# Attention banks read ahead of the selection rounds, fewer filler products, and a token table in two parts

## The reference, cut to what matters

```python
# mixer of the first block: a sparse half and a stick-breaking half
score = einsum(relu(q_idx . k_idx), w_idx); _, idx = top_k(score, 128)   # per query
logits over those keys -> softmax -> @ v_a -> @ w_uv                      # y_a
z = q_b . k_b / 8                                                         # 8 heads, causal
log_a = log_sigmoid(z) + reverse_cumsum(log_sigmoid(-z)) - log_sigmoid(-z)
y_b = exp(log_a) @ v_b
merged = sigmoid(gate_a) * (y_a @ w_o_a) + sigmoid(gate_b) * (y_b @ w_o_b)

# mixer of the second block: gated recurrence hm, differential attention ha, then [hm, ha] @ w_out

# experts of the second block: 32 experts in 4 groups, two experts per token
y = sum over the two experts of weight * ((silu(x @ w_gate[e]) * (x @ w_up[e])) @ w_down[e])
```

## Time and profile before

| what | value |
|---|---|
| median of 3 runs | 1993.67 us (1993.01 to 1994.95) |
| the profiled execution's own time | 1993.76 us |
| span in its profile | 1991.9 us |
| granted TensorE clock, mean | 0.992 |
| busy: PE, DVE, ACT | 96%, 52%, 35% |
| chain that ended last | PE 73%, DVE 10%, DMA 10%, ACT 5% |

### The profile page before, as it was taken

How to read it: one execution, slowest core, us unless ns; L and a number is a source line. 1 busy time by engine, 2 the same in 40 slices (tenths; PEclk the granted TensorE clock), 3 DMA queues, 4 the chain that set the end, 5 groups by cost and what they waited for, 6 DMA issues and landing times.

```text
span 1991.9 us, 22020 instructions
## 1 busy us (share of the span) xinstructions
PE 1909.5 (96%) x8839; PEld 1380.6 (69%) x8839; DVE 1044.3 (52%) x1690; ACT 699.7 (35%) x1139; POOL 42.1 (2%) x67
## 2 busy tenths in 40 slices
PE   7999999998999989999999999999999999998998
PEld 6888888875778867888888878877676444443433
DVE  5443554467777886544334447565765333332333
ACT  5321323345556364332222234565542111111111
POOL 0000000100000001000000000000000000000000
PEclk9999999999999999999999999999999999999999
DMA  5323334134223304333233333222168999999997
GB/s 172 102 87 103 98 96 112 46 80 59 76 64 75 106 27 135 92 95 102 85 106 95 96 94 97 75 64 57 60 238 353 421 420 420 420 421 420 420 422 292
DMA packets 256302, 338.65 MB, mean 170 GB/s; under 512 B 10001, under 2 KB 218897, under 8 KB 232641
## 3 DMA queue, kind: packets, MB, share of 16 engines
q1 hardware_dynamic: 249744, 320.71, 46.9%
q0 software_dynamic: 5872, 15.41, 2.1%
q10 hardware_dynamic: 576, 1.05, 0.1%
HBM read 332.74 MB, written 8.39 MB: 171 GB/s over the span
## 4 chain that ended last, share of the span: by engine, by line
PE 73%; DVE 10%; DMA 10%; ACT 5%; issue 1%; SPq 0%; DVEq 0%; ACTq 0%
PE bank L183 72%; DMA large<-w_up 10%; PE bank L186 1%; ACT wH L189 1%; ACT p L189 1%; ACT T L189 1%; DVE PTL L195 1%; DVE y L195 1%; DVE p L198 0%; DVE score L201 0%; DVE score L219 0%; DVE st L207 0%; DMA stage<-w_gate 0%; ACT rr L189 0%; DVE top L216 0%
## 5 line engine op out<-in xcount | busy, mean ns | idle before, releaser
L183 PE MATMUL bank<-hH,wH 128*128 128x512 f32 x1096 | 433.8, 396 | 16.4 <-DVE stage0L L195 12.1
L183 PE MATMUL bank<-hL,wH 128*128 128x512 f32 x1096 | 428.3, 391 | 0.0
L189 ACT ACTIVATE wH<-stage 128x1024 fp32r<-128x1024 f32 (+3 forms) x231 | 228.4, 999 | 98.7 <-PE bank L183 84.6
L183 PE MATMUL bank<-large,xF 128*64 128x512 f32 x1024 | 236.6, 604 | 18.7 <-DMA large<-w_up 16.8
L183 PEld LDWEIGHTS bank<-hH,wH 128*128 128x128 f32 x1096 | 206.9, 189 | 62.2 <-DVE stage0L L195 12.1
L183 PEld LDWEIGHTS bank<-hL,wH 128*128 128x128 f32 x1096 | 206.9, 189 | 43.7 <-issue 1.7
L183 PEld LDWEIGHTS bank<-large,xF 128*64 128x64 f32 x1024 | 75.4, 139 | 150.2 <-issue 143.1
L183 PE MATMUL bank<-hidH,wH 128*128 128x512 f32 x352 | 137.4, 390 | 2.1 <-DVE stage2L L195 0.9
L183 PE MATMUL bank<-hidL,wH 128*128 128x512 f32 x352 | 137.0, 389 | 0.0
L195 DVE TENSOR_TENSOR yoL<-bank,yoH 64x512 fp32r<-64x512 f32 x64 | 44.1, 689 | 148.7 <-ACT yoH L189 147.7
L183 PE MATMUL bank<-large,hF 128*64 128x512 f32 x512 | 116.0, 595 | 0.0
(11 more groups left out here) (494 smaller groups left out, 3352.9 us busy)
## 6 DMA issues: line engine op xcount, KB each, us to landing
large<-w_gate SPq DMA_DIRECT2D x64, 1024.0 KB, 26.8
large<-w_up SPq DMA_DIRECT2D x64, 1024.0 KB, 26.7
large<-w_down SPq DMA_DIRECT2D x64, 1024.0 KB, 26.7
stage<-w_in SPq DMA_DIRECT2D x56, 512.0 KB, 4.1
stage<-w_gate SPq DMA_DIRECT2D x44, 512.0 KB, 3.7
stage<-w_up SPq DMA_DIRECT2D x44, 512.0 KB, 3.7
stage<-w_down SPq DMA_DIRECT2D x16, 512.0 KB, 3.5
stage<-w_out SPq DMA_DIRECT2D x12, 512.0 KB, 4.1
```

The lines of the kernel that those rows point to most:

```text
L183: return self.e.matmul(*a, **k) if self.e is not None else Nothing()
L189: return self.e.activation(*a, **k) if self.e is not None else Nothing()
```

## The change

In the first mixer the list is reordered: rounds of `topk` that stood between a projection and the read of its bank are moved behind the read, in equal number within each part of the list. The read of gate 7 before head 3 gets an `evict()` of its own ahead of `qk(2, 1)`. `b3(4)` moves behind `qk(3, 1)` and the split of head 5. `b1` of an even head waits only for the even k buffer. The constant products of `b1` go, those of `expand(0)` go from 13 to 6, and `values(0)` moves ahead of `logits(4)`. In the second mixer the weights are prepared three units early instead of two in one `fill`. For the experts, the table of token numbers becomes a product of its own that waits for fewer DVE operations, in bank 1, and the row scales and weights are a second product behind project(0,1), in bank 6. `extras` uses another tile. The second `fetch` no longer waits for `ei` but for `rs`. The transposes of blocks 2 and 3 move into the middle of down(0), and DVE's part of them ahead of that of down(0).

```diff
@@ mixer1
-                left.append(Step("split_qk", ..., y=gts.take(("qk", c, which)), ...))
+                left.append(Step("split_qk", ..., y=gts.take(("qk_odd", c) if which else ("qk", c)), ...))
             score(3, 1, low4)
-            topk(1)
             qk(0, 1, 7)
-            topk(1)
             evict()
-            topk(1)
+            topk(2)
             gate(5)
-            topk(2)
+            topk(3)
             b1(0)
...
             part("b1_max", 1)
-            topk(2)
-            evict()
             topk(1)
             part("b1_split", 1)
+            evict()
             b3(0)
-            topk(1)
+            b3_split(0)
             qk(1, 1, 7)
-            b3_split(0)
             evict()
             part("b2", 1)
-            topk(1)
+            topk(4)
             part("b2_exp", 1)
...
             part("b2_exp", 2)
             part("b2", 2)
+            evict()
             topk(1)
             part("b2_split", 2)
             b1(3)
             part("b1_log", 3)
             qk(2, 0, 6)
             b3(2)
-            topk(2)
             part("b1_max", 3)
+            topk(1)
+            part("b1_split", 3)
             evict()
             b3_split(2)
-            part("b1_split", 3)
-            topk(1)
             qk(2, 1, 7)
+            evict()
             part("b2", 3)
-            topk(1)
-            evict()
+            topk(3)
             part("b2_exp", 3)
...
             qk(3, 0, 6)
-            b3(4)
             qk(3, 1, 7)
-            b3_split(4)
             part("b1_max", 5)
             topk(1)
             part("b1_split", 5)
-            topk(1)
             evict()
+            b3(4)
+            b3_split(4)
             part("b2_exp", 5)
-            topk(1)
+            topk(2)
             part("b2_split", 5)
...
             turn_p(2)
+            values(0)
             logits(4)
             evict()
-            values(0)
@@ mixer2, fill
+                ahead[0] = AHEAD + (outs[0] == 6)
                 add_out(outs[0], 0, hm, ("hm", 3))
+                ahead[0] = AHEAD
@@ moe
-            M.xg.slots[1][1] = ("ei",)
+            M.xg.slots[1][1] = ("rs", 1)
...
             project(0, 0)
-            add(Step("table", bank=banks.take(("rs", 1))))
+            ids_bank = banks.take(("tokx",), 1)
+            add(Step("table", bank=ids_bank))
             add(Step("extras"))
...
             project(0, 1)
+            add(Step("table_shares", bank=banks.take(("rs", 1), 6)))
...
+                if n == 0:
+                    turn_x(2)
+                    steps[-1].inside = turned = steps[-1]
+                    fetch(2 + 2 * NGR)
                 down(n)
                 if n == 0:
-                    turn_x(2)
-                    fetch(2 + 2 * NGR)
+                    steps[-1].inside = turned
@@ PE
-                        keep_clock(s.banks[0], {0: 13}.get(n, 0))
+                        keep_clock(s.banks[0], {0: 6}.get(n, 0))
...
-                        keep_clock(s.z[0], {0: 9, 2: 7, 6: 9}.get(n, 0))
                         pe.wait_ge(*after("kb_zero", n % 2))
-                        pe.wait_ge(*after("qk", n // 2, 1))
+                        pe.wait_ge(*after("qk_odd" if n % 2 else "qk_even", n // 2))
+                        pe.wait_ge(*after("qk", n // 2))
...
                         for j in range(4):
                             u = s.units[j // 2]
+                            if j == 2 and s.inside:
+                                turn_pair(s.inside)
...
+                        pe.wait_ge(*after("ids_in",))
+                        for k in range(8):
+                            t = pe.matmul(s.bank.t[0:BLK, 0:NB + NX], R["J"][:, k, :], R["ge"][:, k, 0:NB + NX], ...)
+                    elif s.kind == "table_shares":
                         pe.wait_ge(*after("tables_in",))
-                            (64 x 3*47 from R["GE"][:, k, :, 0:NB + NX])
+                            (64 x 2*47 from R["GE"][:, k, 1:3, 0:NB + NX])
@@ DVE, choose / indices / extras
+                then(... R["ge"] = R["B"] * pair ..., "ids_in")
                 then(... R["Br"] = R["B"] * rcol ...)
-                then(... R["ge"] = R["B"] * pair ...)
                 shares(M)
-                then(... R["B"] = R["Br"] * w12 ..., "tables_in")
...
                 then(dve.tensor_copy(M.tokx[:, :], tf[:, NB:]), "tokx")
+                then(... R["B"] = R["Br"] * w12 ..., "tables_in")
...
-                (rs copied from the same bank)
+            def row_shares(s, M):   # waits for table_shares, then copies rs
...
-                le = R["GE"]...
+                le = M.oh[:, 0:NX * 32]...
+                dve.wait_ge(*after("mm", "first", 1))
```

More of the change, by code:

```diff
@@ L91, in __init__ @@
         self.kind = kind
-        self.key = self.unit = self.bank = self.y = self.gain = None
+        self.key = self.unit = self.bank = self.y = self.gain = self.inside = None
         self.n = self.m = self.k = self.i = 0
@@ L546, in qk @@
                 b = dense(steps, ("qk", c, which), wcols("w_in", (520, 1032)[which] + c * 128, 128), 8, h, ("qkf", c, which), None, n)
-                left.append(Step("split_qk", n=c, k=which, bank=b, y=gts.take(("qk", c, which)), held=("mm", "b1", 2 * c - 1) if c else ("sc", 3, 7)))
+                left.append(Step("split_qk", n=c, k=which, bank=b, y=gts.take(("qk_odd", c) if which else ("qk", c)), held=("mm", "b1", 2 * c - 1) if c else ("sc", 3, 7)))
             def vb_rows(kk):
@@ L1862, in mixer2_stage, with turn_pair @@
                         pe.matmul(s.bank.t[:, :], mat("ones"), s.sq.t[:, :], start=True, stop=True).then_inc(*did("drms", n))
+            def turn_pair(s):
+                pe.wait_ge(*after("xg%d" % s.xg.at, s.n))
+                rows = s.xg.t[:, :].rearrange("s (c p k) -> s c p k", c=2, k=4)
+                for c in range(2):
+                    free(s.banks[c])
+                    for k in range(4):
+                        t = pe.transpose(s.banks[c].t[:, 128 * k:128 * k + 128], rows[:, c, :, k], mat("ident"))
+                    t.then_inc(*did("mm", "xT", s.n, c))
             def expert_steps(steps):
@@ L1867, in expert_steps @@
                     if s.kind == "turn_pair":
[L1868 to L1874, removed]
+                        if not s.inside:
+                            turn_pair(s)
                     elif s.kind == "turn_x":
@@ L1983, in moe_stage @@
                     elif s.kind == "table":
+                        pe.wait_ge(*after("ids_in",))
+                        free(s.bank)
+                        for k in range(8):
+                            t = pe.matmul(s.bank.t[0:BLK, 0:NB + NX], R["J"][:, k, :], R["ge"][:, k, 0:NB + NX], start=k == 0, stop=k == 7)
+                        t.then_inc(*did("mm", "table"))
+                    elif s.kind == "table_shares":
                         pe.wait_ge(*after("tables_in",))
@@ L1987, in moe_stage @@
                         for k in range(8):
-                            t = pe.matmul(s.bank.t[0:BLK, 0:3 * (NB + NX)].rearrange("p (a n) -> p a n", a=3), R["J"][:, k, :], R["GE"][:, k, :, 0:NB + NX],
+                            t = pe.matmul(s.bank.t[0:BLK, 0:2 * (NB + NX)].rearrange("p (a n) -> p a n", a=2), R["J"][:, k, :], R["GE"][:, k, 1:3, 0:NB + NX],
                                           start=k == 0, stop=k == 7)
-                        t.then_inc(*did("mm", "table"))
+                        t.then_inc(*did("mm", "table_shares"))
                     elif s.kind == "fold":
@@ L2756, in mixer1_stage @@
                             dve.wait_ge(*after("qkh", n, 0))
-                            low(M.qb[1][:, :], s.y.t[:, :], M.qb[0][:, :], 0.125).then_inc(*did("qk", n, 0))
+                            low(M.qb[1][:, :], s.y.t[:, :], M.qb[0][:, :], 0.125).then_inc(*did("qk", n))
                         else:
@@ L3065, in indices @@
                 then(dve.tensor_copy(M.tokx[:, :], tf[:, NB:]), "tokx")
+                then(dve.tensor_tensor(R["B"][:, :, :], R["Br"][:, :, :], wide(R["w12"][:, :], [128, 8, NB + NX]), ALU.mult), "tables_in")
                 for half in range(2):
                     then(dve.tensor_copy(M.tp[BLK * half:BLK * half + BLK, :], tf[:, half:NB:2]))
+            def row_shares(s, M):
+                dve.wait_ge(*after("mm", "table_shares"))
                 for half in range(2):
-                    dve.tensor_copy(M.rs[BLK * half:BLK * half + BLK, :], s.bank.t[0:BLK, (NB + NX) * (1 + half):(NB + NX) * (2 + half)]).then_inc(*did("rs", half))
+                    dve.tensor_copy(M.rs[BLK * half:BLK * half + BLK, :], s.bank.t[0:BLK, (NB + NX) * half:(NB + NX) * (1 + half)]).then_inc(*did("rs", half))
             def extras(M):
-                le = R["GE"][:, :, :, :].rearrange("p a c b -> p (a c b)")[:, 0:NX * 32].rearrange("p (a b) -> p a b", b=32)
+                le = M.oh[:, 0:NX * 32].rearrange("p (a b) -> p a b", b=32)
+                dve.wait_ge(*after("mm", "first", 1))
```

(2 more changed lines are left out.)

6 lines of the change are left out of this document (2 added, 4 removed).

## The result

| what | before | changed |
|---|---|---|
| median | 1993.38 us (4 runs, 1993.01 to 1994.95) | 1980.68 us (4 runs, 1979.06 to 1981.36) |
| profiled execution, its span | 1993.76, 1991.9 us | 1979.06, 1977.1 us |

The ratio is 0.9932, with a 95% interval of 0.992 to 0.9945. The change is faster by 12.7 us where 18.7 were forecast; 1980.7 lies inside the range of 1970.5 to 1983 and 5.7 us above the point of 1975.0. The profiled execution is the fastest of the four and gained 14.8 us of span. In a later session of five executions the changed kernel had 1978.08 beside 1993.76. So the sum is first taken against the trace, and the rest is the spread between executions, which the experiments come back to.

What follows compares the result with a forecast made beforehand. PE, broken by DVE and ACT, was taken to bound the kernel up to 1749 us, then loads. Terms 14.1 + 1.0 + 0.9 + 2.7 = 18.7 us gave 1975.0 us; own range 1971 to 1979, stated range 1970.5 to 1983.

Steps and rivals of the forecast that it cites:

- the rivals: Clock falls (0.12), expert stage gives nothing (0.12), DVE bounds the head phase (1982 us, 0.08), slower by delayed splits (1998 us, 0.04).
- signs named for "wrong": Granted clock 0.5 behind any head's start, PE idle by T0L or T1L ahead of b2 or b3, or second DMA hole unchanged.
- the head phase: First mixer: heads start earlier as PE's waits, constants and slow clock go; 14.1 us gained, bounds about 5 and 16.4.
- DVE's walk: First mixer: DVE's new order walked with earlier durations; heads 0, 2, 4 at 499.0, 534.2, 571.3 us, earlier by 2.4, 5.3, 10.8.
- 36.2 us of PE lead to 607.5, DVE has k ready at 607.2: Step for head 6, first mixer: it starts at 607.5 us without waiting, 14.1 us earlier.
- first rival: First mixer: the clock falls at the even heads and at expand(0), price 4 x 2.2 plus 0.9, total 1984.7 us; chance 0.12.
- the row with 1.27 us: PE's wait for T1L ahead of head 1's b2 in the old trace; products still start 0.23 us apart after it.
- expand(0): First mixer: with values(0) first its product comes 2.5 us earlier, but the stretch is DVE's; 1.0 us gained, bounds 0 and 2.5.
- Second mixer: PE's 0.74 us wait for stage3L behind seven constants shortens, haL then sets it; 0.9 us gained, bounds 0 and 1.2.
- Experts: Expert stage: earlier table lets loads start sooner, closing most of the second DMA hole; 2.7 us gained, bounds 0.5 and 4.1.
- the first hole stays, the second closes but for 1.4 us: Low-rate stretches of the expert stage's DMA stream, 1520 to 1524 and 1528 to 1536 us, worth 3.1 and 4.1 us.
- the transposes inside down(0): Expert stage: they free PE of 3.4 us, counted as nothing because DMA is saturated from 1540 us on.

Runs made afterwards that it cites:

- e10: The kernel before with only the head phase of the change (order of reads and rounds, no constants in b1): 1984.06 us, ratio 0.995.
- e9: The kernel before with only the experts' part of the change (table in two parts, transposes inside down(0)): 1990.98 us, ratio 0.9985.
- e6: The changed kernel without the added reads of gate 7 ahead of qk(2,1): 1987.39 us, ratio 0.9964.
- e4: The changed kernel with the whole expert stage as before (one table of three parts, transposes behind down(0)): 1981.5 us, ratio 0.9943.
- e2: The changed kernel with b3(4) ahead of qk(3,1), its split ahead of head 5's, and one selection round moved behind the reads: 1979.91 us, ratio 0.993.
- e3: The changed kernel with values(0) behind logits(4) and 13 constants ahead of expand(0), as before: 1979.3 us, ratio 0.9933.
- e7: The changed kernel with the transposes of blocks 2 and 3 behind down(0) again, table still in two parts: 1981.76 us, ratio 0.9938.
- e1: The changed kernel again, no edit: 1978.08 us, ratio 0.993.
- e5: The changed kernel with the constant products of b1 again (9, 7 and 9 ahead of heads 0, 2 and 6): 1981.59 us, ratio 0.9945.
- e12: e11 without the added constants ahead of heads 2 and 4 and of the merge: 1974.24 us, ratio 0.9903.
- e11: e8 without the five constants at turn_p(3), and with the gate's read ahead of logits(4): 1975.24 us, ratio 0.9906.
- e8: e2 with constants added: 4 ahead of heads 2 and 4, 5 ahead of turn_p(3), 5 ahead of the merge; 1976.93 us, ratio 0.9916.

## Why the prediction was right, and where it was not

**Right in sign and in mechanism, with three of four terms within 1 us.** Where the gain lies (heads, then experts) is confirmed by each part alone: 9.8 us for the heads (e10) and 2.9 for the experts (e9). Undoing a part in a trace answers likewise: 6.1 us at head 4 (e6), 1.7 at the end of the stream (e4). But 1980.7 lies outside the forecast's own range of 1971 to 1979. It is inside the stated one only because that was widened for the rivals, two of which came true in part: DVE bound the even heads more than walked (idle of PE 0.38, 1.25, 1.24 and 1.92 us, forecast 0.7, 0.8, 0.7 and 0), and the clock fell in three places. One of the signs named for "wrong", a low clock behind a head's start, is there at head 6.

**The term that failed: the head phase, 14.1 forecast, 10.1 in the trace.** Up to head 4 DVE's walk holds within 0.6 us (gains 2.6, 5.0 and 10.2, forecast 2.4, 5.3 and 10.8). The step that failed is "36.2 us of PE lead to 607.5, DVE has k ready at 607.2". DVE's k was ready at 608.4, 1.2 later than walked, and I had walked only q and k: the bank that `b1(6)` writes is freed by a split which the diff moves behind exactly these reads. Of the 2.5 us lost at head 6 about 0.6 is head 4's own delay (PE is free at 608.1 in place of 607.5), 0.4 more is DVE's k, and 1.5 the bank. A lowered clock behind the 1.92 us of idle then cost 1.5 more (the gain falls from 11.6 at head 6 to 10.1). e2 moves that one split and gets the 1.5 of the bank and 1.4 of the clock back in its trace. In e3 and e7, with the same wait and no fall, head 7's product with v comes 12.1 and 12.4 us earlier than in the kernel before.

**The clock.** The first rival priced falls at the even heads and at expand(0). At heads 2 and 4, with 1.24 to 1.26 us of idle and no constants, the clock was 1.00 in all 17 cases of nine traces (changed, e1 to e5, e7, e10, e12), and at head 2 of e6 too. At head 6, with 1.92 to 1.94 us, it fell in five of seven (changed, e1, e4, e6, e10; not in e3 and e7). So there the argument from the row with 1.27 us held, and what failed was the length of the idle that I had foreseen at head 6. Behind the heads the rival was right where it spoke of expand(0): 0.62 in 688 to 692. There, where PE has less to do, shorter idles were enough: 1.24 us in e11, and at the merge 1.38 to 1.40 us in four of twelve traces (changed, e6, e7, e9). By the rule of the Trainium skill that was weighed (TensorE: Matmul & The Clock Gate, A second HAM failure mode: psum-queue depth-cycling) brief idles between groups, frequent enough, would do it. The traces agree in the sparse half, with idles of 0.8 to 1.7 us every few us; in the dense head phase idles of 1.25 us did not do it and single ones of 1.9 mostly did. That constants guard against it isn't shown: e5 has them and head 7's product comes 2.7 us later, e12 has none ahead of the heads and is the steadiest.

**expand(0): 1.0 forecast, about 0.6 over eleven traces.** Its product comes 12.7 us earlier where the heads gave 10.1, but most of it is only that the wait moves: 1.6 us for the gate's bank behind it, which no term had. e11 and e12 take it away.

**Second mixer: 0.9 forecast, 0.9 measured** (18.88 us from the last norm's products at 1456.25 and 1446.34 to the first with ha, now 18.00).

**Experts: 2.7 forecast.** 3.6 by the first two traces, 2.9 by the times of e9, 1.7 by the trace of e4. Over all traces the last load ends 446.0 to 448.0 us behind the one-hot products with the new order (eleven traces, mean 446.5) and 447.8, 447.9 and 449.7 with the old one (e4, e10, before; mean 448.5), so about 2.0. The holes are the right quantity, but "the first hole stays, the second closes but for 1.4 us" was only half right: the holes that are left are worth 2.0 and 0.4 us (6 us at 283 GB/s, 8 at 401). In the kernel before the second had been deepened by a table at a lowered clock (0.62 in 1524 to 1528). Why the first was deeper there, 3.1 us, isn't known, since it lies ahead of that table, and the two holes shrank by 4.8 us in sum where the end moved by 3.6. That the transposes inside down(0) are worth nothing is borne out by e7's trace.

**What stays open.** The changed kernel's nine executions lie between 1977.3 and 1984.2 us (median 1979.1), e2's between 1975.3 and 1982.0, e12's within 0.8. The slower ones come mostly with a lower mean clock (e1: 1984.2 at 0.990, its other four at 0.994), so falls of the clock are likely what adds up to 6 us. The slower executions of the changed kernel and e2 have no trace, but the slowest ones of e6, e9 and e11 do. They show falls at the merge (2.5 us over e1 in e6, 2.7 over the kernel before in e9) and at the one-hot products, where e6 and e11 lose 2.0 and 1.2 us by the end of the stream against e1:

```profile
1495.00:1499.00 4.00, 3.52 (x18) 3.53 (x19) 3.51 (x20) 0.40 (x2) 0.00 (x0) 0.57 1.00 420
```

Such falls come in one execution and not in the next, and a comparison of two medians takes them in. That the gate's read behind `logits(4)` brings the slow executions on is suggested by e11 and e12 (read first, spreads 1.7 and 0.8), but e8 has it late and a spread of 2.7. With four and five executions each this isn't settled. The kernels of different sessions were also compared only through the kernel before.

## What to carry to other kernels

When a step is moved, list what it frees as well as what it makes: here a split moved behind two reads held a bank, and the cost was found at a head two steps on, at an engine that doesn't touch the split. Filler products don't cover a wait for the bank they would write to; they only lengthen it. When executions spread by more than the effect, compare start times of one instruction over several traces: eleven traces gave a term of about 0.6 us that no set of five times could. And take in every trace that has the same code at the place, since the ones left out may be those that spread.

## What the runs showed of the hardware

The same idle doesn't always bring the clock down. Behind 1.92 to 1.94 us of idle at the same instruction the granted clock, a mean of the levels 0.50 and 1.00, was 0.57 to 0.66 over 4 us in four traces of the same head phase and 1.00 in two (e3, e7). 4.33 us of idle (e6) gave 0.50. A fall behind that wait at head 6 cost 1.4 to 1.6 us. At the merge 1.38 to 1.40 us of idle gave 0.50 to 0.62 over the 4 us behind it in four traces and 1.00 in eight, and a fall cost 1.2 to 2.7 us. At the one-hot products, with 1.04 and then 0.60 to 0.61 us of idle shortly ahead, the clock was 0.57 to 0.59 over 4 us in three of fourteen traces (e6, e10, e11). In the dense head phase 18 idles of 1.24 to 1.26 us brought no fall. So the length of the idle alone doesn't decide it.
